# Gate and up products of a mixture-of-experts kernel: f16 halves with the weights as the stationary operand

## The reference, cut to what matters

```
padded = (counts + MOE_BLK - 1) // MOE_BLK * MOE_BLK
...
def expert_block(args):
    xb, e = args
    return (jax.nn.silu(xb @ w_g[e]) * (xb @ w_u[e])) @ w_d[e]
```

## Time and profile before

| | us |
|---|---|
| runs of the kernel before (3) | 2752.47, 2752.85, 2755.39 (median 2752.85) |
| the profiled execution, whole | 2750.93 |
| its span, first to last instruction | 2749.3 |
| mixer, until the first gate matmul | about 1330 |
| experts, from there | about 1420 |

### The profile page before, as it was taken

The page is one execution under the profiler, slowest core; times in us unless marked ns, Lnnn a source line. Parts: engine busy times, 40 slices in busy tenths (PEclk is TensorE's granted clock), DMA queues, the critical chain, the costliest instruction groups (busy, mean ns, idle before and its releaser), DMA issues.

```text
span 2749.3 us, 49924 instructions
## 1 busy us (share of the span) xinstructions
PE 2643.6 (96%) x14252; PEld 1820.9 (66%) x14253; DVE 1716.2 (62%) x3920; ACT 1391.3 (51%) x3046; POOL 798.8 (29%) x825
## 2 busy tenths in 40 slices
PE   4999999999999999996699999999999999999997
PEld 2455555555555555553588888888888888888886
DVE  5677777777777777776454455545655444546633
ACT  7666555565555566553344445445545333435533
POOL 1122323232322222331232333323223323333232
PEclk9999999999999999998799999999999999999999
DMA  8376555556655555656556677667767665667763
GB/s 315 82 166 166 156 160 158 152 157 165 163 152 160 154 156 164 166 138 167 187 169 189 186 236 244 200 196 224 235 186 232 205 183 153 194 180 237 235 181 54
DMA packets 546395, 495.22 MB, mean 180 GB/s; under 512 B 411787, under 2 KB 411948, under 8 KB 545340
## 3 DMA queue, kind: packets, MB, share of 16 engines
q1 hardware_dynamic: 517516, 406.08, 49.2%
q0 software_dynamic: 28848, 88.77, 13.8%
HBM read 309.74 MB, written 87.88 MB: 145 GB/s over the span
## 4 chain that ended last, share of the span: by engine, by line
PE 89%; DVE 3%; DMA 3%; ACT 2%; issue 1%; SPq 1%; POOL 1%; POOLq 0%; DVEq 0%; ACTq 0%
PE psB L1676 15%; PE psA L1676 15%; PE psG L574 11%; PE psF L1676 7%; PE psG L1676 7%; PE psE L574 6%; PE psF L574 6%; PE psD L574 6%; PE psC L574 6%; PE psH L574 3%; PE psC L1684 1%; PE psD L1684 1%; PE psE L1691 1%; DMA xg<-hn_rows,slots 1%; DMA slots<-slot_table 1%
## 5 line engine op out<-in xcount | busy, mean ns | idle before, releaser
L574 PE MATMUL psG<-wi_all,both_xT 128*128 128x512 f16 x1536 | 345.2, 382 | 10.9 <-DMA both_xT<-x 10.9
L574 PEld LDWEIGHTS psG<-wi_all,both_xT 128*128 128x128 f16 x1536 | 148.7, 98 | 188.2 <-DMA both_xT<-x 11.1
L1600 POOL DMA_INDIRECT xg<-hn_rows,slots x80 | 99.2, 1240 | 544.0 <-DMA slots<-slot_table 389.4
L1676 PE MATMUL psB<-up_hi,gT_hi 128*128 128x512 f32 x632 | 254.4, 402 | 0.0
L1676 PE MATMUL psA<-gate_hi,gT_hi 128*128 128x512 f32 x632 | 247.3, 391 | 3.1 <-ACT gT_hi L1796 1.7
L1812 DVE TENSOR_TENSOR down_lo<-wi_all,down_hi 128x512 fp32r<-128x512 f32 x256 | 157.0, 686 | 147.1 <-ACT down_hi L1770 147.1
L1676 PE MATMUL psB<-up_hi,gT_lo 128*128 128x512 f32 x632 | 247.6, 392 | 0.0
L1676 PE MATMUL psA<-gate_hi,gT_lo 128*128 128x512 f32 x632 | 247.3, 391 | 0.0
L1676 PE MATMUL psA<-gate_lo,gT_hi 128*128 128x512 f32 x632 | 247.0, 391 | 0.0
L1676 PE MATMUL psB<-up_lo,gT_hi 128*128 128x512 f32 x632 | 246.4, 390 | 0.0
L1796 ACT ACTIVATE gT_hi<-psC 128x512 fp32r<-128x512 f32 x80 | 47.8, 597 | 384.8 <-PE psC L1684 384.8
(11 more groups left out here) (320 smaller groups left out, 5777.2 us busy)
## 6 DMA issues: line engine op xcount, KB each, us to landing
wi_all<-in_w_gate SPq DMA_DIRECT2D x32, 2048.0 KB, 9.5
wi_all<-in_w_up SPq DMA_DIRECT2D x32, 2048.0 KB, 12.9
wi_all<-in_w_down SPq DMA_DIRECT2D x32, 2048.0 KB, 11.7
xt<-in_x SPq DMA_DIRECT2D x32, 512.0 KB, 3.7
um<-u_rows SPq DMA_DIRECT2D x64, 256.0 KB, 2.7
out_rows<-h SPq DMA_DIRECT2D x32, 512.0 KB, 3.0
xres<-in_x SPq DMA_DIRECT2D x31, 512.0 KB, 4.1
hn_rows<-xres SPq DMA_DIRECT2D x31, 512.0 KB, 2.9
```

What stands on the lines that cost most here:

```text
L574: m = nc.tensor.matmul(ps, left[:, l, k, :], weights.half(r, k, n, width), start=(k == opens and j == 0), stop=(k == closes and j == 2))
L1600: pool.indirect_dma_start(xg[:], None, hn_dram, bass.IndirectOffsetOnAxis(ap=slots[:, 0, 0:1], axis=0), bounds_check=SEQ + P - 1).then_inc ...
L1676: m = nc.tensor.matmul(ps[:, :], l[:, k, :], r[:, r_k[n], :], start=(n == 0 and j == 0), stop=(n == len(l_k) - 1 and j == 2))
```

## The change

Gate and up are computed from f16 halves of scaled operands, and the weights become the stationary operand: 192 matmuls per block with 128 moving columns each replace 48 with 512 columns. The output (activation columns by rows) has the layout that the down product needs, so the four transposes L1691 go. For the f16 range each weight matrix gets a power of two as scale: ACT sums the absolute values of gate and of up of the next expert, POOL takes the largest over the partitions, DVE makes the scale in five small steps. The halves of gate and up are kept twice (for this expert and the next), the splits use 2 pieces of 2048 columns in place of 8 of 512, gate and up of the next expert are split in this expert's second block, and every expert has at least two blocks. The down product stays in fp32r.

```diff
-    hi = {n: sb(f"{n}_hi", [P, 8, 512], F32R) for n in raw}
-    lo = {n: sb(f"{n}_lo", [P, 8, 512], F32R) for n in raw}
+    hi = {n: [sb(f"{n}_hi_{p}", [P, 8, 512], F16) for p in range(2)] for n in SCALED}
+    lo = {n: [sb(f"{n}_lo_{p}", [P, 8, 512], F16) for p in range(2)] for n in SCALED}
+    hi["down"], lo["down"] = ([sb(f"down_{w}", [P, 8, 512], F32R)] * 2 for w in ("hi", "lo"))
...
+    CHUNKS = 2
...
-        step(v.tensor_scalar(blocks_of[:, counts], blocks_of[:, E:], 1, None, ALU.max))
-        step(v.tensor_scalar(blocks_of[:, 0:1], blocks_of[:, 0:1], 2, None, ALU.max))
+        step(v.tensor_scalar(blocks_of[:, counts], blocks_of[:, E:], 2, None, ALU.max))
...
             for n in raw:
-                sp.wait_ge(hi_s[n], 8 * e)
-                sp.wait_ge(lo_s[n], 8 * e)
+                sp.wait_ge(hi_s[n], CHUNKS * e)
+                sp.wait_ge(lo_s[n], CHUNKS * e)
                 load_expert(sp, n, e)
...
+        def bound_of(e, p):
+            pool.wait_ge(summed, 2 * (e + 1))
+            hold(pool, held)
+            pool.partition_all_reduce(most(p), sums(p), P, RMAX).then_inc(most_s, 1)
...
+            if isinstance(i, int) and i == 1 and not last:
+                bound_of(e + 1, 1 - p)
...
+        def columns_mm(ps, name, p):
+            for j in range(KE):
+                at = slice(j * P, (j + 1) * P)
+                for k in range(KD):
+                    for t, (w, x) in enumerate(((hi, gT_hi), (hi, gT_lo), (lo, gT_hi))):
+                        m = nc.tensor.matmul(ps[:, at], w[name][p][:, k, at], x[:, k, :], start=(k == 0 and t == 0),
+                                             stop=(k == KD - 1 and t == 2))
+            return m
...
+            columns_mm(psA, "gate", p).then_inc(gate_ps, 1)
             if not static0:
-                turn_act(b)
-            split_mm(psB, range(KD), (gT_hi, gT_lo), (hi["up"], lo["up"]), list(range(KD)), first, "up", e
-                     ).then_inc(up_ps, 1)
+                pe.wait_ge(act_s, b)
+            if first:
+                weights("up", e)
+            columns_mm(psB, "up", p).then_inc(up_ps, 1)
             transpose_rows(b + 1)
...
+        def sum_up(n, e, p, junk):
             act.wait_ge(raw_in[n], 16 * (e + 1))
+            s.activation(junk, raw[n].rearrange("p k n -> p (k n)"), ACT.Abs, accum_out=sums(p, n)).then_inc(summed, 1)
+        def sum_next(n, e, p, b):
+            if not (isinstance(b, int) and b == 0):
+                act.wait_ge({"gate": gate_ps, "up": up_ps}[n], b)
+            sum_up(n, e + 1, 1 - p, hi[n][1 - p][:].rearrange("p k n -> p (k n)").bitcast(BF16))
+        def split(n, e, p):
+            act.wait_ge(step_s, SCALE_STEPS * (e + 1))
+            for c in range(CHUNKS):
+                s.activation(chunk(hi[n][p], c), chunk(raw[n], c), ACT.Copy, scale=power(p, n)).then_inc(hi_s[n], 1)
...
+        def block_(e, i, b, p, last):   # ACT
+            if not (known and b < 2):
+                copy_y(b)
+            if first and not last:
+                sum_next("gate", e, p, b)
+            if not (known and b == 0):
+                turn(b)
+            silu(b, p)
+            if first and not last:
+                sum_next("up", e, p, b)
+            if second and not last:
+                split("gate", e + 1, 1 - p)
+            turn_x(b + 1)
+            if first:
+                split_down(e, b)
+            if second and not last:
+                split("up", e + 1, 1 - p)
...
+        for c, n in enumerate(SCALED):
+            sum_up(n, 0, 0, wi_flat[:, 12288 + c * 2048:12288 + (c + 1) * 2048].bitcast(BF16))
         mixed(act)
...
+        def block_(e, i, b, p, last):   # DVE
+            if not (known and b < 2):
+                copy_y(b)
+            if second and not last:
+                scales(e + 1, 1 - p)
+            if not (known and b == 0):
+                turn(b)
+            if second and not last:
+                split("gate", e + 1, 1 - p)
+            product(b, p)
+            turn_x(b + 1)
+            if first:
+                split_down(e)
+            if second and not last:
+                split("up", e + 1, 1 - p)
```

More of the change, by code:

```diff
@@ L177, in build @@
         rows_of_y = ksb("rows_of_y", [P, 1], I32)
+        rt_stat = ksb("rt_stat", [P, 9], F32)
+        own = ksb("own", [P, 2, 12], F32)
         with ExitStack() as ctx:
@@ L1559, in experts, with walk, expert @@
     gate_ps, up_ps, silu_s, act_s = sem("gate_ps"), sem("up_ps"), sem("silu_s"), sem("act_s")
-    aT_ps, aT_hi_s, aT_lo_s, y_ps = sem("aT_ps"), sem("aT_hi_s"), sem("aT_lo_s"), sem("y_ps")
+    aT_hi_s, aT_lo_s, y_ps = sem("aT_hi_s"), sem("aT_lo_s"), sem("y_ps")
     y_act, y_dve, added, cleared = sem("y_act"), sem("y_dve"), sem("added"), sem("cleared")
     named = sem("named")
[L1564 to L1585, removed]
+    SCALE_STEPS = 5
+    def walk(eng, block):
+        def expert(e, p, last=False):
+            n = eng.value_load(blocks_of[0:1, bass.ds(e, 1)], min_val=2, max_val=TILES)
+            base = eng.value_load(blocks_of[0:1, bass.ds(e + E, 1)], min_val=0, max_val=4 * TILES)
+            start = 0 if isinstance(e, int) and e == 0 else base
+            block(e, 0, start, p, last)
+            block(e, 1, start + 1, p, last)
+            with eng.If(n > 2):
+                with eng.Fori(2, n) as i:
+                    block(e, i, start + i, p, last)
+            return base + n
+        expert(0, 0)
+        with eng.Fori(0, (E - 2) // 2) as pair:
+            expert(pair * 2 + 1, 1)
+            expert(pair * 2 + 2, 0)
+        return expert(E - 1, 1, True)
     def sync(sp):
@@ L1637, in block_ @@
             gather()
-            if known:
+            if known and b < 2:
                 pool.wait_ge(cleared, 3)
@@ L1799, in scalar, with scales, step @@
         s.preload_act_table_set("silu_and_others")
+        for c, n in enumerate(SCALED):
+            sum_up(n, 0, 0, wi_flat[:, 12288 + c * 2048:12288 + (c + 1) * 2048].bitcast(BF16))
         mixed(act)
         act.sem_inc(y_act, 3)
-        halves(act, split, copy_y, silu, turn, turn_x)
+        split("gate", 0, 0)
+        turn_x(0)
+        split("up", 0, 0)
+        total = walk(act, block_)
+        copy_y(total)
+        turn(total)
+        copy_y(total + 1)
     def vector(dve):
         v = nc.vector
-        def split(n, e):
-            dve.wait_ge(raw_in[n], 16 * (e + 1))
-            for k in range(8):
-                dve.wait_ge(hi_s[n], e * 8 + k + 1)
-                v.tensor_tensor(lo[n][:, k, :], raw[n][:, k, :], hi[n][:, k, :].bitcast(F32),
-                                ALU.subtract).then_inc(lo_s[n], 1)
+        def scales(e, p):
+            dve.wait_ge(most_s, e + 1)
+            done = [0]
+            def step(ins):
+                done[0] += 1
+                ins.then_inc(step_s, 1)
+                dve.wait_ge(step_s, SCALE_STEPS * e + done[0])
+                hold(dve, held)
+            bits, floor = own[:, p, 4:6].bitcast(I32), own[:, p, 6:8].bitcast(I32)
+            step(v.tensor_scalar(bits, most(p).bitcast(I32), 0x7F800000, None, ALU.bitwise_and))
+            step(v.tensor_scalar(floor, bits, float(30 << 23), None, ALU.max))
+            step(v.tensor_scalar(power(p).bitcast(I32), floor, -1.0, float(268 << 23), ALU.mult, ALU.add))
+            step(v.tensor_scalar(inverse(p).bitcast(I32), floor, float(-(14 << 23)), None, ALU.add))
+            step(v.tensor_scalar(inverse(p), inverse(p), inv_hn, None, ALU.mult))
+            assert done[0] == SCALE_STEPS
@@ L1845, in vector @@
         dve.sem_inc(y_dve, 3)
-        halves(dve, split, copy_y, product, turn, turn_x)
+        split("gate", 0, 0)
+        turn_x(0)
+        split("up", 0, 0)
+        total = walk(dve, block_)
+        copy_y(total)
+        turn(total)
+        copy_y(total + 1)
     return dict(sync=sync, tensor=tensor, scalar=scalar, gpsimd=gpsimd, vector=vector)
```

143 lines of the change are left out of this document (73 added, 70 removed).

## The result

The changed kernel takes 2954.57 us (median of 4 runs, 2950.55 to 2957.81) against 2753.05 for the kernel before beside it. The ratio is 1.073, with a 95% interval of 1.071 to 1.075. The prediction was 2772, in a range of 2722 to 2850: slower was right, the size was not. Some 200 us are to be found, and the forecast had 19 of them.

A forecast was written before the change was run, and what follows sets the result against it. PE's matmuls were taken to bound the expert stage. Matmuls -52, late sums +63, rows +9 and the last block's transposes -1 gave +19 on 2750.9, 2770, or 2772 for the runs' median; range 2722 to 2850.

The forecast's parts named there:

- The matmuls: Gate and up on PE: 56 ns per 128-column matmul, a block of 17.05 us, gain 0.66 per block, 52 us over 79.
- The rival that narrow matmuls don't stream: PE in long runs: queue or weight load binds, up to 98 ns a pair, 2870 to 3340 us; chance 12%.
- The late up sum: PE's second block behind two-block experts waits for turn_x behind ACT's up sum: 3.7 us, 17 times, +63 us.
- The rows: PE waiting for gathered rows: 0.6 us for each of 15 three-block experts, +9 us.
- POOL's step in front of the gather: POOL's largest-of-partitions step waits for the second sum, slot load and gather behind it: nothing, or up to 1 us in 16 places.
- the chain: POOL's copy_y, scatter, slot list and gather: some 24 us, no shorter while blocks shorten; +9 us of PE waiting for rows.
- The clock: PE at half clock after a stall, 2 us more each: nothing taken, 17 x 2 = 34 us kept for the range.
- The start: Before the first expert's blocks: sums of expert 0 lie beside the end of the mixer, no cost taken.

The follow-up runs named there:

- the rolled kernel: Changed kernel with the four column groups of gate and of up as a register-addressed loop of four turns on PE: 3301.47 us, 1.200.
- the kernel with two copies and the orders of the change: Changed kernel with only PE's loop over expert pairs altered, two copies of the block in place of six: 2848.34 us, 1.035.
- the three moves: Against wide f16 (2847.5 us): ACT's sums behind turn and turn_x, DVE's scales before its down split, POOL's largest-over-partitions step behind the next gather: 2742.52 us, 0.997.
- the kernel before with its walk in pairs: Kernel before with the change's walk, two experts a turn, six block copies on PE: 2757.12 us; with 18 copies in PE's loop: 2774.09 us.
- small loads: Changed kernel with the weight loads of experts 1 to 31 cut from 2 MB to 32 KB each: 2810.38 us, 1.021.

## Why the prediction was wrong, point by point

**The matmuls** were right: 17.09 us a block against 17.05, 55.8 ns a matmul against 56, over 192 in every block. The rival that narrow matmuls don't stream is dead. The Trainium skill, TensorE: Matmul & The Clock Gate, section Back-to-back issue gap, has 81 ns for such a stream; the trace does not agree. Something like it came only with register instructions between, 80 ns in the rolled kernel.

**The late up sum** was right in place, count and nearly in size. Its clean measurement is the kernel with two copies and the orders of the change: 17 stalls at the gate product, 1.1 to 6.5 us, 70.8 in all; predicted were 17 x 3.7 = 63. In the changed kernel itself it hardly shows, since the larger stalls cover it. The prices of ACT's sum (3.62 + 0.19 against 3.65 + 0.15), and of the split pieces (2.0 and 2.35 us against 2.0 and 2.3) held.

**The rows** were under-sized. The step was "nothing, or up to 1 us in 16 places" for POOL's step in front of the gather, and +9 for the chain. With two copies PE waits 25 us for rows, and the three moves together, POOL's step among them, bring that to 15. The queue behind a waiting instruction was named, and its price taken at its lower end.

**The clock** was sized wrongly: "I take nothing". Rows of the mixer in the prediction had shown the half clock after 18 us of idle; here it follows much shorter idles as well, all of 3.8 us and more before a gate product and some from 1.9 us on (see the last section). In the kernel with two copies and the orders of the change, 14 gate products are longer for it, 28 us in all, near the 34 kept in the range; in the changed kernel it is 40 us in 20.

**The start** was taken as free ("the sums of expert 0 lie beside the end of the mixer"). The first gate product comes at 1337.8 in place of 1329.8, 8 us later. Half of it is the new step on POOL: it ran at 1326.17, though the sums had been ready since 1320.0, and the first slot load stood behind it (9.4 us after POOL's last instruction of the mixer, in place of 5.4). The other half was there before: the last matmul of the mixer ended at 1311.91 in place of 1308.27, and no run isolates why.

These terms alone (-49 + 71 + 25 + about 35 for the clock in all products, + 8) make 90, and the kernel with two copies measured 95. With them the prediction would have had some 2843, near the upper edge of its range; the kernel with two copies took 2848.

**What was missing** is the other 106 us. The step that failed lies before the sum: the change was costed as matmuls, waits and transfers, and the program that PE has to hold was not costed at all. The diff shows 192 unrolled matmuls for 48 and six copies of a block in a loop; the page before shows a queue called "instruction" with 14 packets. Multiplying the two would have given the question. The runs put it beyond the late sums: only PE's loop was changed between 2896.4 and 2736.9, and packets fell from 200 to 19. That it is PE's own instructions that the packets bring isn't seen in a row; but the packets rise and fall with PE's loop alone, from 19 to 88 in the kernel before with its walk in pairs and from 200 to 19 in the changed one, whose 50,625 matmuls and weight loads are the same in both.

A page bears on this that the prediction did not use. The Trainium skill, Runtime: NRT & Kernel Launch, section Instruction fetch mechanics, says that PE's instruction memory holds 2048 instructions, is refilled in blocks of 16 KiB or 256 instructions, in sequence, and that a taken branch whose target is outside the current window of two blocks must wait for a fetch. The trace agrees with the block: 3.28 MB in 200 packets are 16.4 KB each. It agrees that sequence is hidden and jumps are not. It does not agree with a window of two blocks: loops of 896 and 1008 instructions turned with 19 packets and without such idles. With the 2048 it agrees roughly: 2688 and 3024 do not stay, but 1792 did not either (151 packets). These counts are of matmuls and weight loads; waits and register instructions add 64 to the 2688 of a turn with six blocks.

What a wait costs is seen in the runs. With small loads it is 1.4 to 2.1 us for one jump and 6.1 to 7.2 for two in a row; with the 2 MB loads about 4 over the third copy, 1.6 to 3.8 back to the start, and 10.9 to 12.9 for both.

Not settled: why two jumps in a row take three times as long as one. That a prefetch begun for the first target has to end before the second can start would fit, and no run tried it.

## What to carry to other kernels

Before unrolling, multiply: instructions a copy times copies in the loop, matmuls and weight loads both. Here a loop of 1008 on PE stayed, and one of 1792 was fetched again in every turn, with stalls at its jumps; nothing between was tried. Above some 1000, look at the packets of the instruction queue on the page, which tell it in one number, and if they rise, loop over blocks in place of copying them. A sum over data that has just been loaded belongs behind whatever feeds PE on its own engine, and the step on POOL that needs it behind the next gather. Moving only ACT's sum of up made it worse; the three moves were run only together.

## What the runs showed of the hardware that was not expected

The kernel with two copies and the orders of the change, windows of 3 us behind an idle of 3.69 us (ended 1735.51) and behind one of 2.48 us (ended 1694.06), and below them the changed kernel behind an idle of 2.42 us (ended 2388.64) and behind one of 2.99 us (ended 2496.96):

```profile
1735.50:1738.50 3.00, 2.99 (x29) 3.00 (x30) 2.44 (x2) 3.00 (x4) 0.80 (x2) 0.50 0.01 0
1694.10:1697.10 3.00, 3.00 (x55) 3.00 (x56) 2.49 (x2) 3.00 (x4) 0.60 (x1) 1.00 0.01 0
...
2388.60:2391.60 3.00, 2.96 (x40) 3.00 (x41) 0.69 (x1) 1.85 (x3) 1.64 (x1) 0.72 0.79 191
2497.00:2500.00 3.00, 3.00 (x55) 3.00 (x56) 0.69 (x1) 1.47 (x3) 1.75 (x2) 1.00 0.58 175
```

- In the first pair the longer idle was followed by half clock (29 matmuls), the shorter by the full one (55). In the second pair it is the other way round: clock 0.72 and 40 matmuls behind 2.42 us, 1.00 and 55 behind 2.99. So the length of the idle alone doesn't decide. Over all runs but the rolled one, and leaving out the first gate product, no idle of up to 1.89 us before a gate product was followed by half clock, all from 3.8 us on were, and between the two either came; what decides there stays open. A stretch at half clock made its gate product 1.2 to 3 us longer.
- A queue of large loads lengthens a fetch of instructions: idles of 6.1 to 7.2 us at two jumps in a row with small loads, 10.9 to 12.9 with 2 MB loads.
- 128-column f16 matmuls with their own weight load (98 ns each) run at 55.8 ns in every block without a stall, 192 to a block; with register instructions between them it is 80.
- The change can be made to pay, if little: 2736.85 us, 0.994 of the kernel before. Of the 0.62 us that a block gains (49 us in 79), 16 come through: the first gate product comes 9 us later (1339.0), and PE's idle time in the stage is 21 us longer, 15 of it for rows.
